# Leaving out the products of ones that nobody reads, at seven norms and in a layer norm

## The reference

```python
def rmsnorm(x, g):
    xf = x.astype(jnp.float32)
    y = xf * lax.rsqrt(jnp.mean(xf * xf, axis=-1, keepdims=True) + EPS)
    return (y * g.astype(jnp.float32)).astype(x.dtype)

def layernorm(x, g, b):
    xf = x.astype(jnp.float32)
    mu = jnp.mean(xf, axis=-1, keepdims=True)
    var = jnp.mean(jnp.square(xf - mu), axis=-1, keepdims=True)
    y = (xf - mu) * lax.rsqrt(var + EPS)
    return (y * g.astype(jnp.float32) + b.astype(jnp.float32)).astype(x.dtype)
```

## Time and profile before

| | |
|---|---|
| time, median of 3 (lowest, highest) | 3342.81 us (3339.97, 3347.37) |
| profiled execution: time, span | 3345.9 us, 3343.6 us |
| mean granted clock of TensorE in it | 0.989 |
| busy: PE, PEld, DVE, ACT | 97%, 74%, 59%, 34% |
| DMA | 370.04 MB, mean 111 GB/s |

### The profile page before, as it was taken

One profiled execution on the slowest core, in us unless ns is written; L12 is line 12 of the kernel. 1 busy time (PEld: TensorE's weight loads), 2 busy tenths in 40 slices (PEclk: granted clock), 3 DMA queues, 4 the chain that ended last, 5 costly groups with the idle time before them and its releaser, 6 DMA issues. The chain is left out here.

```text
span 3343.6 us, 39117 instructions
## 1 busy us (share of the span) xinstructions
PE 3242.1 (97%) x14052; PEld 2489.0 (74%) x14052; DVE 1969.8 (59%) x2761; ACT 1145.3 (34%) x1545; POOL 103.7 (3%) x172
## 2 busy tenths in 40 slices
PE   5999999999899999999999999999999999999999
PEld 2446788887678888767888876688887758888887
DVE  7885765535668864565766367676645554455523
ACT  3224422225532222444433231443333353252222
POOL 1000001000001100000000010000000100000000
PEclk9998999999999999999999999999999999999999
DMA  8222465541125543212222335222233222223232
GB/s 305 90 69 82 140 199 194 162 136 67 51 101 200 190 150 94 82 44 82 95 94 93 97 100 141 67 86 99 91 98 138 70 76 83 100 82 101 94 96 87
DMA packets 105053, 370.04 MB, mean 111 GB/s; under 512 B 11664, under 2 KB 11664, under 8 KB 104688
## 3 DMA queue, kind: packets, MB, share of 16 engines
q1 hardware_dynamic: 83696, 289.02, 26.6%
q0 software_dynamic: 20096, 75.38, 6.8%
q10 hardware_dynamic: 1152, 4.19, 0.3%
HBM read 357.80 MB, written 2.10 MB: 108 GB/s over the span
## 5 line engine op out<-in xcount | busy, mean ns | idle before, releaser
L2419 DVE TENSOR_TENSOR weight_lo<-weight_ring,weight_hi 128x1024 fp32r<-128x1024 f32 (+1 forms) x473 | 571.7, 1209 | 926.2 <-ACT weight_hi L1668 919.3
L1668 ACT ACTIVATE weight_hi<-weight_ring 128x1024 fp32r<-128x1024 f32 (+1 forms) x473 | 494.6, 1046 | 1590.7 <-PE proj_banks L940 977.6
L940 PE MATMUL proj_banks<-h_lo,weight_hi 128*128 128x512 f32 x1672 | 651.2, 389 | 0.0
L940 PE MATMUL proj_banks<-h_hi,weight_hi 128*128 128x512 f32 x1312 | 510.5, 389 | 0.4 <-DVE weight_lo L2419 0.4
L940 PE MATMUL proj_banks<-h_hi,weight_lo 128*128 128x512 f32 x1312 | 510.4, 389 | 0.0
L940 PEld LDWEIGHTS proj_banks<-h_lo,weight_hi 128*128 128x128 f32 x1672 | 314.2, 188 | 64.8
L940 PEld LDWEIGHTS proj_banks<-h_hi,weight_hi 128*128 128x128 f32 x1312 | 246.2, 188 | 52.4 <-issue 0.8
L940 PEld LDWEIGHTS proj_banks<-h_hi,weight_lo 128*128 128x128 f32 x1312 | 246.3, 188 | 51.2
L940 PE MATMUL proj_banks<-mid_hi,weight_hi 128*128 128x512 f32 x704 | 273.9, 389 | 0.0
L940 PE MATMUL proj_banks<-mid_lo,weight_hi 128*128 128x512 f32 x704 | 273.9, 389 | 0.0
L940 PE MATMUL proj_banks<-mid_hi,weight_lo 128*128 128x512 f32 x704 | 273.9, 389 | 0.0
(11 more groups left out here) (428 smaller groups left out, 5142.2 us busy)
## 6 DMA issues: line engine op xcount, KB each, us to landing
weight_ring<-in_w_up SPq DMA_DIRECT2D x176, 512.0 KB, 3.3
ada_ring<-in_ada POOLq DMA_DIRECT2D x96, 512.0 KB, 3.7
weight_ring<-in_w_dn SPq DMA_DIRECT2D x64, 512.0 KB, 3.5
weight_ring<-in_w_br SPq DMA_DIRECT2D x32, 512.0 KB, 3.2
weight_ring<-in_w_upr SPq DMA_DIRECT2D x32, 512.0 KB, 3.3
weight_ring<-in_w_dnr SPq DMA_DIRECT2D x32, 512.0 KB, 3.3
weight_ring<-in_w_dn SPq DMA_DIRECT2D x32, 384.0 KB, 3.1
cond<-in_ada POOLq DMA_DIRECT2D x20, 512.0 KB, 4.6
```

What stands on the lines that cost most here:

```text
L940: last = mm(proj.banks[:, u % RING, :], stationary(home + n)[:, w], moving(k), start=k + m == 0, stop=k == kt - 1 and m == 2)
L1668: return nc.scalar.activation(out, in_, func, **kw)
L2419: return v.tensor_tensor(out, a, b, op)
```

## The change

All calls of `keep_clock` and `hold_clock` go, and with them the two functions: three times three matmuls of 256 columns at each of norms 1 to 7, and two and seven matmuls of 512 columns in the layer norm. The banks that these calls opened are opened by the first matmul that is read, as they were before for the same key.

```diff
     def first_three(name, r, lo):
 
         split0, third = c.first_split[name], list(THIRD).index(r)
-        keep_clock(open_bank(proj, (name, 0)))
         for k in range(KD):
...
-    def hold_clock(bank, count):
-
-        for _ in range(count):
-            mm(bank, c.square("ones"), c.sq_const[:, 0:S], start=True, stop=True)
-
-    def keep_clock(bank):
-
-        for _ in range(3):
-            mm(bank[:, 0:2 * P], c.square("ones"), c.sq_const[:, 0:2 * P], start=True, stop=True)
-
     def norm(r):
 
         n = stat_count(r)
-        if r > 0:
-            keep_clock(open_bank(mix, ("ss", r)))
         if r == 0:
...
             row_sums(r, T(SQ0 + KD - 1), False, True)
-        if r > 0:
-            keep_clock(open_bank(mix, ("bc", r)))
         pe.wait_ge(s["rstd_ready"], r + 1)
         spread_rows(r, 1)
...
     sum_squares(("lnm", 0), u_ready, u_tile, KD, first=7)
-    hold_clock(open_bank(mix, ("lnv", 0)), 2)
     sum_squares(("lnv", 0), lambda k: (s["u_sq"], k + 1), lambda k: T(SQ0 + k), KD)
-    hold_clock(open_bank(proj, ("cout", 0)), 7)
     for k in range(KD):
```

## The result

The changed kernel takes 3354.27 us in the median of 13 runs against 3344.15 us of the kernel before, 13 runs: ratio 1.0031, 95% interval 1.0023 to 1.0039, 10.1 us slower. One of the 13 took 4525 us at a mean granted clock of 0.678; the ratio leaves it out. One execution of its own was profiled, with a span of 3352.4 us and a mean granted clock of 0.983, against 3343.6 us and 0.989.

A forecast was written before the change was run, and what follows sets the result against it. TensorE, busy 97%, was taken to bound the kernel. Six norms +15.6, norm 6 +0.1, layer norm +2.8 and cover -1.0 gave +17.5 us: 3363.4 us, 3360 as the median, range 3348 to 3373.

The forecast's parts named there:

- Removed work gains nothing but at norm 6: Of 38.7 us of ones removed, only 1.1 us, at norm 6, delays later work; the rest fills waits, gain 0.
- The clock falls at each of norms 1 to 7: Without ones, sparse TensorE work lowers the clock at each norm: 2.6 us each, +15.6 us for six norms.
- the chain: Row sums and spread at a norm run slower at the low clock: 0.7 us a norm, bounds 0 and 1.2.
- the products: The products of first_three behind a norm start at the low clock: 1.9 us a norm, low bound 1.0.
- Norm 6: Block on the path gone -1.1, slower spread +0.7, slower products behind ssc +0.5: sum +0.1 us, bounds -1.1 and +1.4.
- The layer norm, +2.8: Square sums +1.9, first cout steps +1.2, a later low stretch perhaps missed -0.3; bounds 0.6 and 4.8 us.
- Cover behind, -1.0: Later waits for a split weight give back some lost time: -1.0 us in all, bounds 0 and -3.
- B: Norms keep their clock and only the layer norm pays: +1.7 us, 3344.5 us; chance 0.11.
- C: The clock falls early at every norm and stays down longer: +29.6 us, 3372 us; chance 0.09.
- D: The third block holds back the first product at seven norms; removal gains 10.2 us, 3333 us; chance 0.03.
- E: The clock falls but later waits absorb it, under 6 us in all: 3346 us; chance 0.03.
- the signs: Expected in the changed profile: PE busy time down about 30 us, low clock around norms, mean clock some 0.983.

The follow-up runs named there:

- first_two: The kernel before with the third block of ones left out at norms 1 to 7, the first two blocks kept; ratio 0.9997.
- third_of_ones: The kernel before with one matmul of ones instead of three in each of the three blocks at a norm; ratio 1.0011.
- ln_off: The kernel before with only the ones of the layer norm left out; 3343.9 us, ratio 0.9999.
- norms_off: The kernel before with only the ones at the norms left out, those of the layer norm kept; 3352.94 us, ratio 1.0024.
- third_only: The kernel before with the first two blocks of ones left out at the norms, the third kept; ratio 1.0013.
- after_shift: The changed kernel with two matmuls of ones (1.7 us) added in the dense products behind norm 1; 3355.15 us, ratio 1.0041 to the kernel before.
- early_shift: The kernel before with two matmuls of ones (1.7 us) added ahead of the product gv, near 100 us; 3335.64 us, ratio 0.9979.
- more_ones: The kernel before with ones added ahead of nine more waits and the third block left out at norm 6; 3333.94 us, ratio 0.9983.

## Why the prediction was right in direction and in part in size

*Removed work gains nothing but at norm 6.* Shown: the waits kept their releasers and distances, and first_two gained 1.29 us at norm 6 where 1.1 was forecast.

*The clock falls at each of norms 1 to 7.* Shown, by the clock in the windows of the changed kernel and by first_two and third_of_ones, in which the cost comes and goes with the low stretch. Sum for six norms: forecast +15.6, measured 2.25 + 2.32 + 3.82 + 2.80 + 2.26 + 2.44 = +15.9, each within the bounds of 1.3 and 3.9. At norm 1 the part of the chain is +0.9 (forecast 0.7) and that of the products +1.3 (forecast 1.9). This split differs from norm to norm: the chain pays nothing at norm 4 and 0.9 at norms 1, 3 and 5, 3.7 over the six (forecast 4.2), the products 1.3 to 2.9 us, 12.2 over the six (forecast 11.4). The prediction said that no single idle time at a norm passes 1.7 us; at norm 4 one of 1.84 us came out. Norm 6: forecast +0.1, measured +0.4.

*The layer norm, +2.8.* Sums +1.68 (forecast 1.9) and cout +0.99 (forecast 1.2) are near; the low stretch of the earlier trace rows, for whose going I took -0.3, went altogether: -1.61. Net +1.1. That stretch is not the layer norm's own: it is gone in ln_off, and also in norms_off (13.73 us) and first_two (13.70), which leave the layer norm as it was, while third_only and third_of_ones keep it (15.32 and 15.31). The -0.3 stood for a chance, and which way it went was luck.

*Cover behind, -1.0.* This term was mis-sized, and the prediction's reason covers only a part of it. 15.9 + 0.4 + 1.1 = 17.4 us were lost at the places named (17.3 before rounding), 13.9 are left at the end: 3.5 were given back. The matched matmuls show where. Some 1.9 us came back in the first 25 us behind norms 1, 2 and 3 (0.4, 0.4 and 1.1), 1.2 of it in waits for a low half of the input (h_lo) and 0.7 at a split weight, the kind of wait that the prediction named. This one, of the kernel before:

```profile
988.66 0.47 PE L940 MATMUL proj_banks<-h_hi,weight_hi 128*128 128x512 f32 x1 [0.44 <-DVE weight_lo L2419]
```

In the changed kernel the same matmul starts without a wait. Another 1.8 us came back between norms 4 and 5, where the kernel before has four low stretches (at 1452.6, 1480.0, 1507.3 and 1531.2 us, 13.7 us in all) and the changed one two (1482.3 and 1509.6, 10.2 us). This is what after_shift shows at another place, and the prediction had no term for it. The other stretches add up to some +0.3.

*The sum against one execution.* +17.5 us was forecast; the medians say +10.1. The traces put a difference of 13.9 behind norm 1 and -5.1 ahead of it, where the two kernels have the same instructions. The prediction had no term for that part. The times of the kernel before tend to two groups: of 27 runs beside the first four experiments, 13 lie between 3337.1 and 3342.3 and 14 between 3345.2 and 3347.1, and of the 63 beside the later ones 8 lie between the groups. All three traces are of the upper, so that the sum was made against an execution of the upper group. The time goes with the mean granted clock: of these 90 executions none at 0.991 took more than 3339.8 us, and none at 0.988 less than 3346.1. Why an execution gets the one or the other was not settled, as none of the lower group was traced; early_shift shows only that norm 1 can come 7 us earlier after a shift of 1.7. Of the 8.7 us by which the traces' difference of 8.8 misses the +17.5, then, 5.1 lie ahead of norm 1, and 3.6 behind it: 2.5 in the cover and 1.7 in the layer norm, less 0.6 that the norms lost beyond their forecast.

*The rivals.* B is refuted by norms_off and by the clock at the norms. C is wrong in size: only norm 3 came near 3.9. D is refuted by the distances at the norms. E, that what is lost is absorbed, holds for 3.5 of 17.4 us. As for the signs: the busy time fell by 25.5 us instead of 30, since what remained of the work ran longer. The mean clock came out at the 0.983 that was forecast, partly by luck: the forecast was 40 us more at the low clock, and the changed kernel has some 58 us of it at the places named and some 18 us less at others.

## What to carry to other kernels

Work that nobody reads can be what keeps TensorE's clock up: before leaving it out, look at the granted clock where it stands, count what the engine would do there without it, and price the products that follow at the low clock (here 8 of them in 3.4 us, 1.6 us lost). Filling work (the ones here) paid only where it could start when the wait did, so its bank has to be free by then (more_ones), and where it ended before what was waited for (the third block of norm 6 did not, and cost 1.3 us). And a kernel whose clock falls at many waits can answer to a shift of 1.7 us with nothing or with several us (both were met here), so differences of that size are read place by place in matched traces, not from the total.

## What the runs showed of the hardware

- Behind 180 us a low stretch of 3.4, 6.8, 10.2 or 13.7 us was met (at 394.2 us in third_only, 390.1 and 966.9 in the changed kernel, 318.9 in first_two).
- The same idle time did not always have the same outcome: 1.84 us ahead of the first product at norm 4 in first_two was followed by the low clock, 1.90 us with 0.17 us of work in it elsewhere was not the earlier trace rows, and at the other five of the six norms of first_two, with 1.50 to 1.66 us there, the clock did not fall.
- What each norm costs repeats between the two traces of the changed kernel to within 0.03 us, and the kernel made 1.7 us later was within 0.6 us of the same places after 440 us of work.
- 1.7 us of work that nobody reads, added near 100 us, made the kernel faster, ratio 0.9979 (0.9967 to 0.9992).
- Executions of the kernel before at a mean granted clock of 0.991 took 3337.1 to 3339.8 us, those at 0.988 3346.1 to 3350.1.
